# Two-stage ConvFFN in a decoder step: a due-time order of VectorE's work at stage and round changes, a new opening with the norm's sums in job 0 and the last squares summed on TensorE

## The chip, the cores and the metric

One core of one Trainium2 chip runs the whole step. The metric is the device time of one execution in microseconds, the median of several. Names in the profile: PE (TensorE), DVE (VectorE), ACT (ScalarE), POOL (GpSimd), SP (the queue that issues the DMAs).

## The reference

Two layers of a decoder trunk for 1024 prompt tokens and 8 x 8 sample tokens (1088 columns, model width 1024), in float32. Layer 0 has an attention and RG-LRU mixer, layer 1 a chunked mixer; after each mixer stands the part that the change touches:

```python
def rmsnorm(x, g):
    y = xf * lax.rsqrt(jnp.mean(xf * xf, axis=-1, keepdims=True) + EPS)
    return (y * g.astype(jnp.float32)).astype(x.dtype)
...
def conv_ffn(xn, buf, w_g, w_u, w_c, b_c, w_d):
    g = xn @ w_g                                   
    gc, new_buf = causal_dwconv(g, buf, w_c, b_c)  
    return (jax.nn.gelu(gc) * (xn @ w_u)) @ w_d, new_buf
```

`yp = yp + f_p` adds the result to the residual x. The norm's gain is folded into x before the products, its scale `rsqrt(...)`, one number per column, comes after them (`rms_scale`).

## The kernel before, in words

Activations lie with the model width on the partitions (8 tiles of 128 x 1088) and the tokens on the free axis. A float32 operand is split into two fp32r parts, `hi` (rounded, by ACT) and `lo` (the rest, by DVE or POOL), and a product is hi x hi + lo x hi + hi x lo on PE.

**Jobs and products.** An FFN (`class Ffn`) is 40 jobs. Jobs 0 to 23 are stage one: job 2t is a pair of 128 output rows of the gate projection, job 2t+1 the same pair of the up projection. Jobs 24 to 39 are stage two (the down projection): 4 rounds (a round has 6 of the 24 hidden tiles) of 4 quarters (2 output tiles each). Every job is a 2 x 2 block product done with 7 block products instead of 8; their names are `B21, B11, T1, T2, B22, NT4, T3` (0 to 6). The x side of T1, T2, NT4 and T3 are sums of quarters of x, and the weight side are the block sums S1 to S4. A product is 24 matmuls of 128 x 128 x 272 in stage one and 18 in stage two (all L2159, `multiply`), into one of three bank pairs d, a, bb of PSUM; so products wait until the earlier content of their bank is added out.

**Who does what behind PE.** ACT rounds the weight blocks (`block_hi`, L2255), copies bank groups to SBUF (`copy_out`, L2274), does conv bias, gelu (L2303) and the hi parts of the pieces. DVE makes block sums (`block_sum`, L2095) and block low parts (`block_lo`, L2099), adds the other groups (`add_out`, L2466), does the gate scaling by `rms_scale` (`scale_gate`, L2472), the conv taps (L2481), hidden tiles (L2501) and sums (L2511), low parts of the hidden pieces in stage two (`piece_lo`, L2110) and the residual additions (`add_residual`, L2530). POOL does block low parts 0, 1, 5, scales the gelu's result (`gate_scale`, L2105) and adds up the squares (`add_squares`, L1661). Each engine's order is written out by hand; semaphores carry all dependences, and DVE waits in order.

**Opening.** `Output` computes the mixer's output projection, tile by tile (m = 0 to 7), in 12 us each, adds it to x (`vector`, L1828, "evacuation") and spills x to DRAM (`spill_tile`). The first job of the FFN needs all tiles: the B operands (`tile_act`, `tile_dve`, L2393) and the T sums (`open_dve`, `opening_dve`: L2418 for T1, L2398 for T3, L2404 for T2, L2436 for NT4), then hi (ACT) and lo (`part_lo`, L2427 and, on POOL, L2119 and L2124). The squares of the eight tiles are added on POOL into one array, whose column sums are three fp32 matmuls with a matrix of ones (`sums_pe`, L1669); roots follow on ACT (`roots_act`). The product order of job 0 is B11, B21, T1, T2, sums 0 and 1, B22, sum 2, NT4, T3.

**Change of stage.** In stage one x lies in DRAM and its SBUF space holds gate, conv and up tiles. The last hidden pair is finished by DVE at the end of job 24 (`down_first`); SP stores it, then reloads x:

```python
        for g in range(7, 11):
            self.load_piece(sp, g)
        self.store_hidden(sp, PAIRS - 1)
        sp.wait_ge(self.hc, 16 * PAIRS)
        self.reload(sp, 2)
        ...
        self.reload(sp, 3)
        for r in range(ROUNDS):
            ...
            self.load_next(sp, n + 4 * r + 3)
```

The last line with r = 0 loads the w_down block of job 27. In an ordinary job n of stage two DVE first makes S1 and S2 of job n + 1 (`next_sums`), and then adds residual 0, 1, ... of job n. PE's fourth product (T2) of a job waits for residual 1 of the same job, since both use bank a; the first of the next job waits for residual 5.

**Round change.** In the last quarter of a round (jobs 27, 31, 35) and the first of the next (28, 32, 36) DVE also makes the 7 low parts of the next round's hidden pieces.

## Time and profile before

| what | us |
|---|---|
| median of 3 runs | 2572.05 (2571.69 to 2580.36) |
| the profiled execution's own time | 2573.28 |
| its span in the trace | 2571.6 |
| PE busy | 2462.0 (96%) |
| DVE busy | 1769.5 (69%) |
| ACT busy | 1149.9 (45%) |

PE is nearly always busy, so time can only be gained where it is not, or where its granted clock is low. Stretches are given in microseconds from the start of the span. FFN 0 runs from about 590 to 1437, FFN 1 from about 1710 to the end.

### The profile page before, as it was taken

What the parts mean: (1) busy time and instruction counts of PE and PEld (TensorE: products, weight loads), DVE (VectorE), ACT (ScalarE), POOL (GpSimd) and SP (SyncE); (2) the same over time, 40 slices, a digit from 0 to 9 for tenths busy, and PEclk for the clock granted to TensorE, in tenths of its full rate; (3) what the DMA queues carried; (4) which work ended last, traced back from release to release, by engine and by line L of the source; (5) the groups of instructions that cost most, each with busy time, mean ns of one, the idle gap of its engine ahead of it and who ended that gap; (6) DMA issues with size and microseconds to landing.
All of it is one profiled execution on the core that took longest, in us unless ns stands there. A gap on an engine that the chain in (4) does not pass through costs nothing.

```text
span 2571.6 us, 46180 instructions
## 1 busy us (share of the span) xinstructions
PE 2462.0 (96%) x18693; PEld 2361.4 (92%) x18693; DVE 1769.5 (69%) x2158; ACT 1149.9 (45%) x1851; POOL 959.7 (37%) x623
## 2 busy tenths in 40 slices
PE   7999998899899999998999999998999999989998
PEld 7888786589899999998999999997999999989998
DVE  7466557645877777778778443637878787787775
ACT  5565756533544444443334433525444444443331
POOL 3234333214445453542223411334545454532221
PEclk9999999999899999999999999999999999999999
DMA  5101116852222222336443111122232322265422
GB/s 183 52 27 51 40 29 209 270 192 77 84 102 94 98 102 90 111 125 231 141 141 93 47 49 37 52 75 85 91 116 85 107 93 98 89 235 196 140 89 83
DMA packets 214177, 276.99 MB, mean 108 GB/s; under 512 B 11437, under 2 KB 158998, under 8 KB 210894
## 3 DMA queue, kind: packets, MB, share of 16 engines
q1 hardware_dynamic: 212910, 271.83, 31.7%
q8 instruction: 149, 2.44, 0.4%
q10 hardware_dynamic: 576, 2.10, 0.2%
q14 instruction: 62, 0.51, 0.1%
q0 software_dynamic: 480, 0.11, 0.0%
HBM read 203.57 MB, written 70.43 MB: 107 GB/s over the span
## 4 chain that ended last, share of the span: by engine, by line
PE 64%; DVE 9%; issue 3%; ACT 1%; POOL 1%; DMA 1%; DVEq 0%; ACTq 0%; POOLq 0%
PE psum_all L2159 52%; PE psum_all L2823 7%; PE psum_all L148 3%; DVE down_x_ffn L2110 2%; DVE psum_all L2095 1%; DVE x_residual L2530 1%; DMA w_raw<-in_w_gate_dram 1%; PE psum_all L2875 0%; PE psum_all L2839 0%; POOL rms_scale L1661 0%; DVE x_residual L2481 0%; POOL w_lo_part L113 0%; DVE ffn_x_sums L2418 0%; DVE ffn_x_sums L2404 0%; DVE blocks_down L2099 0%
## 5 line engine op out<-in xcount | busy, mean ns | idle before, releaser
L2159 PE MATMUL psum_all<-ffn_x,blocks 128*128 128x272 f32 x5760 | 736.7, 289 | 24.1 <-DVE ffn_x L2427 13.1
L2159 PEld LDWEIGHTS psum_all<-ffn_x,blocks 128*128 128x128 f32 x5760 | 730.1, 189 | 25.7 <-issue 15.0
L2159 PE MATMUL psum_all<-down_x_ffn,blocks_down 128*128 128x272 f32 x2880 | 375.8, 291 | 25.1 <-DVE x_residual L2530 21.5
L2159 PEld LDWEIGHTS psum_all<-down_x_ffn,blocks_down 128*128 128x128 f32 x2880 | 369.1, 191 | 28.3 <-issue 28.1
L2274 ACT COPY x_residual<-psum_all 128x544 f32<-128x544 f32 x192 | 117.9, 614 | 372.9 <-PE psum_all L2159 369.5
L113 POOL TENSOR_TENSOR w_lo_part<-w_raw,w_hi_part 128x1024 fp32r<-128x1024 f32 x52 | 126.9, 2440 | 355.8 <-ACT w_hi_part L97 355.7
L2530 DVE TENSOR_TENSOR x_residual<-x_residual,psum_all 128x544 f32<-128x544 f32 (+1 forms) x224 | 178.4, 798 | 117.8 <-PE psum_all L2159 116.7
L2481 DVE SCALAR_TENSOR_TENSOR x_residual<-x_residual,ffn_params 128x1088 f32<-128x1088 f32 x96 | 215.0, 2240 | 0.0
L2105 POOL TENSOR_TENSOR x_residual<-x_residual,rms_scale 128x1088 f32<-128x1088 f32 x48 | 152.9, 3185 | 151.8 <-ACT x_residual L2303 151.8
L2466 DVE TENSOR_TENSOR x_residual<-x_residual,psum_all 128x544 f32<-128x544 f32 x144 | 130.3, 905 | 91.4 <-PE psum_all L2159 89.5
L2099 DVE TENSOR_TENSOR blocks<-psum_all,blocks 128x512 fp32r<-128x512 f32 x144 | 99.2, 689 | 122.1 <-ACT blocks L2255 122.1
L2823 PE MATMUL psum_all<-operand_a,w_hi_part 128*128 128x364 f32 (+1 forms) x672 | 169.9, 330 | 0.0
L909 PE MATMUL psum_all<-in_hi_even,w_hi_part 128*128 128x384 f32 (+1 forms) x456 | 157.0, 344 | 1.1 <-DVE xb_padded L1430 0.6
L1363 POOL TENSOR_TENSOR take_then_weights<-take_then_weights,x_residual 128x511 f32<-128x511 f32 (+3 forms) x96 | 96.1, 1012 | 156.9 <-DVE x_residual L1395 116.7
L2159 PE MATMUL psum_all<-ffn_x,block_a 128*128 128x272 f32 x1152 | 152.0, 287 | 1.3 <-ACT rms_scale L1676 1.3
L2159 PE MATMUL psum_all<-ffn_x,block_s 128*128 128x272 f32 x1152 | 151.8, 287 | 0.0
L909 PE MATMUL psum_all<-in_lo_even,w_hi_part 128*128 128x384 f32 (+1 forms) x456 | 149.3, 327 | 0.0
L2159 PEld LDWEIGHTS psum_all<-ffn_x,block_a 128*128 128x128 f32 x1152 | 146.9, 188 | 2.4 <-issue 2.4
L909 PE MATMUL psum_all<-in_hi_even,w_lo_part 128*128 128x384 f32 (+1 forms) x456 | 149.1, 327 | 0.0
L2159 PEld LDWEIGHTS psum_all<-ffn_x,block_s 128*128 128x128 f32 x1152 | 146.9, 188 | 0.0
L1395 DVE TENSOR_TENSOR_SCAN x_residual<-x_residual,all_ones 128x512 f32<-128x512 f32 (+3 forms) x96 | 91.9, 991 | 73.2 <-ACT x_residual L1183 73.2
L2511 POOL TENSOR_TENSOR x_residual<-x_residual 128x544 f32<-128x544 f32 x88 | 130.0, 1477 | 6.3
(361 smaller groups left out, 4632.6 us busy)
## 6 DMA issues: line engine op xcount, KB each, us to landing
staging_ffn<-hidden_spill SPq DMA_DIRECT2D x54, 816.0 KB, 5.0
hidden_spill<-x_residual SPq DMA_DIRECT2D x24, 1088.0 KB, 4.0
w_raw<-in_w_gate_dram SPq DMA_DIRECT2D x24, 1024.0 KB, 5.4
x_residual<-in_w_up_dram SPq DMA_DIRECT2D x24, 1024.0 KB, 5.2
pages<-in_cache_k_dram SPq DMA_DIRECT2D x64, 256.0 KB, 3.7
pages<-in_cache_v_dram SPq DMA_DIRECT2D x64, 256.0 KB, 4.5
x_spill<-x_residual SPq DMA_DIRECT2D x24, 546.0 KB, 5.5
x_residual<-x_spill SPq DMA_DIRECT2D x24, 546.0 KB, 6.2
```

The costliest lines, as they stand in the source:

```text
L113: pool.tensor_tensor(dst if dst is not None else self.lo[:, par, :], self.raw[:, par, :], (hi if hi is not None else self.hi[:, par, :]).b ...
L909: mm = pe.matmul(bank(key, 0, b - a), wt[:, n % 2, col], xt[:, k, a:b], start=k == 0 and s == 0, stop=k == KT - 1 and s == 2)
L1363: pool.tensor_tensor(t[:, 0:n - 1], t[:, 0:n - 1], k[:, 1:n], ALU.mult).then_inc(weighted, 1)
L2099: eng.tensor_tensor(self.block(n, i, 1).rearrange("p (q c) -> p q c", c=P), self.source(n, i), self.block(n, i, 0).bitcast(F32).rearrange( ...
L2105: pool.tensor_tensor(self.conv[:, r, :], self.conv[:, r, :], self.core.rb[:, 0:USED], ALU.mult).then_inc(self.gr_ready, 1)
L2159: mm = pe.matmul(self.core.ps[:, b + h, 0:HB], wt[:, q * P:(q + 1) * P], xt[:, q, HB * h:HB * (h + 1)], start=first and at == 0, stop=at = ...
L2274: act.copy(self.half(self.target(n, r), h).rearrange("p (h n) -> p h n", h=2), self.group(name)).then_inc(self.act_out, 1)
L2466: dve.tensor_tensor(dst, dst, src, ALU.add).then_inc(self.dve_out, 1)
L2481: o.did(dve.scalar_tensor_tensor(gc, gb[:, j:j + USED], par[:, f + FT * j:f + FT * j + 1], gc, ALU.mult, ALU.add))
L2511: eng.tensor_tensor(dst, x, y, op).then_inc(self.hsum, 1)
L2530: dve.tensor_tensor(dst, dst, src, ALU.add).then_inc(self.dve_out, 1)
L2823: mm = pe.matmul(self.core.ps[:, self.lane_bank(f), 0:width(c)], wm[:, is_u, col], xm[:, k, chunk(c)], start=k == 0 and s == 0, stop=k == ...
```

## The change

1. **Squares.** The squares of tiles 6 and 7 go to a second array (`late_sq`), those of tile 7 are not added on POOL but by PE: each sum is a matmul of the total and one or two of the last squares, into one bank. Three fp32 matmuls become seven.
2. **Opening.** The product order of job 0 is B11, T1, B21, B22, sums 0 and 1, T2, NT4, sum 2, T3. DVE evacuates tile 6 after two block sums instead of after six block operations; it evacuates tile 7 behind T1's low part. The low parts of T1 and T3, which POOL shared, are all DVE's. Products with `made_first` wait for their low part only at their third group of matmuls. SP spills tiles 4 and 5 ahead of the gate weights of job 0. The waits for all spills become waits for pairs of tiles.
3. **Stage change.** `down_first` goes; job 24 and every first job of a round are `turned_job`, the last of a round `turn_job`. The last hidden tiles and sums are spread over job 25 (`last_hidden`), and both gate scalings of the last pair stand on POOL behind block part 5 in job 24.
4. **Round change.** The low parts of B22, NT4 and T3 come before S1 and S2 of the following job; block low parts 4 and 6 go into the job after.

Of `opening_act`, `open_dve` and `opening_dve` the diff below has the new lines alone.

```diff
...
     def square(self, act, m):
         if m >= 2:
             act.wait_ge(self.s_sum, m - 1)
-        act.activation(self.core.rb[:, 0:USED] if m == 0 else self.sq[:, 0:USED], self.core.x[:, m, 0:USED], ACT.Square
-                       ).then_inc(self.s_sq, 1)
+        act.activation(halves(self.core.rb[:, 0:USED]) if m == 0 else self.square_at(m),
+                       halves(self.core.x[:, m, 0:USED]), ACT.Square).then_inc(self.s_sq, 1)
...
                 self.ffn.spill_tile(sp, m - 4)
+        self.ffn.spill_tile(sp, 4)
+        self.ffn.spill_tile(sp, 5)
         sp.wait_ge(w.s_lo, n0 + KT + 2)
         self.ffn.load(sp, 0)
-        for m in range(4, KT):
-            self.ffn.spill_tile(sp, m)
+        self.ffn.spill_tile(sp, 6)
+        self.ffn.spill_tile(sp, 7)
...
     def vector(self, dve):
         for m in range(KT):
             if m == KT - 2:
-                self.ffn.first_weights_dve(dve)
-            elif m == KT - 1:
-                self.ffn.open_dve(dve)
+                self.ffn.block_sum(dve, 0, "S1")
+                self.ffn.block_sum(dve, 0, "S2")
             dve.wait_ge(*self.job_done(m))
             tile = chunks(self.core.x[:, m, :])
             dve.tensor_tensor(tile, tile, self.bank(m)[:, :, 0:CH], ALU.add).then_inc(self.evac, 1)
-            self.ffn.tile_dve(dve, m, KT - 1)
+            if m < KT - 2:
+                self.ffn.tile_dve(dve, m)
+            elif m == KT - 2:
+                self.ffn.open_dve(dve)
...
+    def square_at(self, m):
+        return self.mem.late_sq if m >= KT - 2 else super().square_at(m)
+
+    def sum_bank(self, c):
+        return self.banks["bb"] if c == 2 else self.banks["d"] + c
+
+    def sums_pe(self, pe, which):
+
+        late = self.square_at(KT - 1)
+        pe.wait_ge(self.s_sum, KT - 2)
+        pe.wait_ge(self.s_sq, KT)
+        for c in which:
+            out = self.core.ps[:, self.sum_bank(c), 0:width(c)]
+            pe.matmul(out, self.core.ones[:, :], self.core.rb[:, chunk(c)], start=True, stop=False,
+                      skip_group_check=True)
+            a, b = c * CH, c * CH + width(c)
+            for h in range(2):
+                lo, hi = max(a, HALF * h), min(b, HALF * (h + 1))
+                if lo < hi:
+                    mm = pe.matmul(out[:, lo - a:hi - a], self.core.ones[:, :], late[:, h, lo - HALF * h:hi - HALF * h],
+                                   start=False, stop=True, skip_group_check=True)
+            mm.then_inc(self.s_mm, 1)
...
-    FIRST_PIECES = {(-1, 4): (B21, B11), (-1, 5): (T1,), (-1, 6): (T2,), (0, 1): (NT4,), (0, 2): (T3,)}
+    FIRST_PIECES = {(-1, 4): (B21, B11), (-1, 5): (T1,), (-1, 6): (T2,), (0, 1): (NT4, T3)}
...
     def sync(self, sp):
-        sp.wait_ge(self.x_out, 16 * KT)
-        sp.wait_ge(self.sum_lead, self.T_MADE[NT4][0])
+        self.x_out(sp, 1)
+        sp.wait_ge(self.sum_lead, self.T_MADE[NT4][1])
         self.load(sp, 1)
...
         self.add_squares(pool, KT - 2)
-        pool.wait_ge(self.act_lead, self.T_HI[T1])
-        pool.tensor_tensor(self.operand(0, T1, 1)[:, 0:2], self.temp(T1)[:, 0:2],
-                           self.operand(0, T1, 0)[:, 0:2].bitcast(F32), ALU.subtract).then_inc(self.t1_lo, 1)
-        self.add_squares(pool, KT - 1)
         self.block_lo(pool, 0, 5)
-        pool.wait_ge(self.act_lead, self.T_HI[T3])
-        pool.tensor_tensor(self.operand(0, T3, 1)[:, 0:2], self.temp(T3)[:, 0:2],
-                           self.operand(0, T3, 0)[:, 0:2].bitcast(F32), ALU.subtract).then_inc(self.t3_lo, 1)
         for n in range(JOBS):
             t = n // 2
             up, last = n < JOBS1 and n % 2, n == JOBS - 1
             for i in range(7):
                 if not last and i in (0, 1, 5):
                     self.block_lo(pool, n + 1, i)
-                if up and (i == 3 or i == 5 and n < JOBS1 - 1):
+                if up and n < JOBS1 - 1 and i in (3, 5):
                     self.gate_scale(pool, t, (i - 3) // 2)
-                elif n == JOBS1 and i == 1:
+                elif n == JOBS1 and i == 5:
+                    self.gate_scale(pool, PAIRS - 1, 0)
                     self.gate_scale(pool, PAIRS - 1, 1)
                 if up and i == 6 and n < JOBS1 - 1:
                     self.hidden_sum(pool, t, T1)
...
+        made_first(T1)
+        pe.wait_ge(self.b_lo, 11)
+        pe.wait_ge(*self.lo_ready(0, 0))
+        self.multiply(pe, 0, 0)
+        pe.wait_ge(self.b_lo, 12)
+        pe.wait_ge(*self.lo_ready(0, 4))
+        pe.wait_ge(self.act_out, 1)
+        self.multiply(pe, 0, 4)
+        pe.wait_ge(self.act_out, 2)
+        self.sums_pe(pe, (0, 1))
         pe.wait_ge(self.dve_out, 1)
-        self.multiply(pe, 0, 3)
-        pe.wait_ge(self.act_out, 1)
-        self.sums_pe(pe, (0, 1))
-        pe.wait_ge(*self.lo_ready(0, 4))
-        pe.wait_ge(self.b_lo, 12)
-        pe.wait_ge(self.act_out, 2)
-        self.multiply(pe, 0, 4)
+        made_first(T2)
+        pe.wait_ge(self.s_root, 2)
+        made_first(NT4)
+        pe.wait_ge(self.dve_out, 2)
         self.sums_pe(pe, (2,))
-        pe.wait_ge(*self.lo_ready(0, 5))
...
+        for i in range(3):
             self.block_hi(act, 0, i)
+        self.tile_hi(act, KT - 2)
+        self.block_hi(act, 0, 3)
         act.wait_ge(self.out.freed, 1)
         for q in range(4):
+            self.even_copy(act, T1, q, 0)
+        act.wait_ge(self.s_sum, KT - 3)
+        self.block_hi(act, 0, 4)
         act.wait_ge(self.out.freed, 2)
+        self.even_copy(act, T3, 0, 1)
+        self.even_copy(act, T3, 1, 1)
+        self.sum_hi(act, T1)
+        self.even_copy(act, T3, 2, 1)
+        self.even_copy(act, T3, 3, 1)
+        self.square(act, KT - 2)
         act.wait_ge(*self.out.job_done(KT - 1))
         self.block_hi(act, 0, 5)
+        self.tile_hi(act, KT - 1)
         self.block_hi(act, 0, 6)
+        self.square(act, KT - 1)
+        self.copy_out(act, 0, 2)
         self.copy_out(act, 0, 0)
+        self.sum_hi(act, T2)
+        self.sum_hi(act, NT4)
+        self.roots_act(act, (0, 1))
...
+    def open_dve(self, dve):
         self.block_lo(dve, 0, 2)
+        self.tile_dve(dve, KT - 2)
         self.block_sum(dve, 0, "S4")
         self.block_lo(dve, 0, 3)
         self.block_sum(dve, 0, "S3")
         for q in range(4):
+            self.t1_sum(dve, q)
+        self.t3_sum(dve, 0)
+        self.t3_sum(dve, 1)
+        self.t2_sum(dve, 0)
+        self.block_lo(dve, 0, 4)
+        self.sum_lo(dve, T1)
+
+    def opening_dve(self, dve):
+        self.nt4_sum(dve, 0)
+        self.tile_lo(dve, KT - 1, 0, B21, 0)
+        self.t3_sum(dve, 2)
+        self.t3_sum(dve, 3)
+        self.tile_lo(dve, KT - 1, 1, B22, 1)
+        for q in (1, 2, 3):
             self.t2_sum(dve, q)
+        for q in (1, 2, 3):
+            self.nt4_sum(dve, q)
         self.add_out(dve, 0, 1)
+        self.sum_lo(dve, T2)
+        self.sum_lo(dve, NT4)
         self.block_lo(dve, 0, 6)
+        self.add_out(dve, 0, 4)
+        self.sum_lo(dve, T3)
...
+    def turn_job(self, dve, n, r):
+
+        self.next_sums(dve, n + 1)
+        self.add_residual(dve, n, 0)
+        self.add_residual(dve, n, 1)
+        self.piece_lo(dve, r + 1, B21)
+        self.add_residual(dve, n, 2)
+        self.piece_lo(dve, r + 1, B11)
+        self.next_lo(dve, n + 1, 2)
+        self.add_residual(dve, n, 3)
+        self.next_lo(dve, n + 1, 3)
+        self.add_residual(dve, n, 4)
+        self.next_lo(dve, n + 1, 4)
+        self.add_residual(dve, n, 5)
+        self.piece_lo(dve, r + 1, T1)
+        self.add_residual(dve, n, 6)
+        self.piece_lo(dve, r + 1, T2)
+
+    def turned_job(self, dve, n, r):
+
+        if r == 0:
+            self.piece_lo(dve, 0, T1)
+        self.add_residual(dve, n, 0)
+        if r == 0:
+            self.piece_lo(dve, 0, T2)
+        self.block_lo(dve, n, 6)
+        self.add_residual(dve, n, 1)
+        self.piece_lo(dve, r, B22)
+        self.add_residual(dve, n, 2)
+        self.piece_lo(dve, r, NT4)
+        self.add_residual(dve, n, 3)
+        self.piece_lo(dve, r, T3)
+        self.block_sum(dve, n + 1, "S1")
+        self.add_residual(dve, n, 4)
+        self.block_sum(dve, n + 1, "S2")
+        self.add_residual(dve, n, 5)
+        self.next_lo(dve, n + 1, 2)
+        self.add_residual(dve, n, 6)
+        self.next_lo(dve, n + 1, 3)
+
+    def last_hidden(self, dve, i):
+        t = PAIRS - 1
+        if i < 2:
+            self.hidden_tile(dve, t, i)
+        elif i < 4:
+            for k in ((T1, T3), (T2, NT4))[i - 2]:
+                self.hidden_sum(dve, t, k)
...
```

The order of the built programs shows three places. The first is DVE's opening of FFN 0, from the last block sums to the evacuation of tile 7 (L1828 before, L1843 now; `ffn_x_sums_7973` is T1, `_7974` T3, `_7975` T2, `_7976` NT4). Before:

```order
L2099 TENSOR_TENSOR blocks<-psum_all,blocks 128x512
L2095 TENSOR_TENSOR psum_all<-w_raw,psum_all 128x512
L2099 TENSOR_TENSOR blocks<-psum_all,blocks 128x512
L2095 TENSOR_TENSOR psum_all<-w_raw 128x512
L1828 TENSOR_TENSOR x_residual<-x_residual,psum_all 128x1092
L2393 SCALAR_TENSOR_TENSOR ffn_x_7964<-x_residual,params,ffn_x_7964 128x544
L2418 SCALAR_TENSOR_TENSOR ffn_x_sums_7973<-x_residual,params,ffn_x_sums_7973 128x544 x4
L2398 SCALAR_TENSOR_TENSOR ffn_x_sums_7974<-x_residual,params,ffn_x_sums_7974 128x544 x3
L2404 SCALAR_TENSOR_TENSOR ffn_x_sums_7975<-x_residual,params,ffn_x_sums_7974 128x544 x3
L1828 TENSOR_TENSOR x_residual<-x_residual,psum_all 128x1092
L2393 SCALAR_TENSOR_TENSOR ffn_x_7963<-x_residual,params,ffn_x_7963 128x544
```

Now:

```order
L1843 TENSOR_TENSOR x_residual<-x_residual,psum_all 128x1092
L2144 TENSOR_TENSOR blocks<-psum_all,blocks 128x512
L2439 SCALAR_TENSOR_TENSOR ffn_x_7964<-x_residual,params,ffn_x_7964 128x544
L2140 TENSOR_TENSOR psum_all<-w_raw,psum_all 128x512
L2144 TENSOR_TENSOR blocks<-psum_all,blocks 128x512
L2140 TENSOR_TENSOR psum_all<-w_raw 128x512
L2455 SCALAR_TENSOR_TENSOR ffn_x_sums_7973<-x_residual,params,ffn_x_sums_7973 128x544 x4
L2444 SCALAR_TENSOR_TENSOR ffn_x_sums_7974<-x_residual,params,ffn_x_sums_7974 128x544 x2
L2450 SCALAR_TENSOR_TENSOR ffn_x_sums_7975<-x_residual,params,ffn_x_sums_7974 128x544
L2144 TENSOR_TENSOR blocks<-psum_all,blocks 128x512
L2468 TENSOR_TENSOR ffn_x_7966<-ffn_x_sums_7973,ffn_x_7966 128x2176
L1843 TENSOR_TENSOR x_residual<-x_residual,psum_all 128x1092
```

The evacuation of tile 6 has moved ahead of four block operations; that of tile 7 had ten tile sums ahead of it, and has now seven, a block part and T1's whole low part (L2468).

The second is DVE in jobs 24 to 26 of FFN 0, around the last hidden tiles (L2501, now L2554) and sums (L2511, now L2564); L2530, now L2583, are residual additions, L2095, now L2140, block sums. Before:

```order
L2530 TENSOR_TENSOR x_residual<-x_residual,psum_all 128x1088
L2099 TENSOR_TENSOR block_s_7980<-psum_all,block_s_7980 128x384
L2501 TENSOR_TENSOR x_residual<-x_residual 128x1088 x2
L2511 TENSOR_TENSOR x_residual<-x_residual 128x544 x4
L2095 TENSOR_TENSOR psum_all<-w_raw 128x384
L2095 TENSOR_TENSOR psum_all<-psum_all,w_raw 128x384
L2530 TENSOR_TENSOR x_residual<-x_residual,psum_all 128x544 x3
L2099 TENSOR_TENSOR blocks_down<-psum_all,blocks_down 128x384
L2095 TENSOR_TENSOR psum_all<-w_raw,psum_all 128x384
```

Now, with the two sums of job 27 and the residuals of job 26 behind them:

```order
L2554 TENSOR_TENSOR x_residual<-x_residual 128x1088
L2583 TENSOR_TENSOR x_residual<-x_residual,psum_all 128x544
L2554 TENSOR_TENSOR x_residual<-x_residual 128x1088
L2583 TENSOR_TENSOR x_residual<-x_residual,psum_all 128x544
L2564 TENSOR_TENSOR x_residual<-x_residual 128x544 x2
...
L2583 TENSOR_TENSOR x_residual<-x_residual,psum_all 128x544
L2564 TENSOR_TENSOR x_residual<-x_residual 128x544 x2
...
L2140 TENSOR_TENSOR psum_all<-pair_raw_ffn_7992 128x384
L2140 TENSOR_TENSOR psum_all<-psum_all,pair_raw_ffn_7992 128x384
L2583 TENSOR_TENSOR x_residual<-x_residual,psum_all 128x544 x3
```

Tiles and sums are spread between the residuals 0 to 3 of job 25; the sums from `pair_raw_ffn` (job 27's w_down) stand in front of job 26's residuals, as they did.

The third is DVE at the first round change, job 28. Before:

```order
L2110 TENSOR_TENSOR down_x_ffn_7990<-staging_ffn_7989,down_x_ffn_7990 128x1632
L2530 TENSOR_TENSOR x_residual<-x_residual,psum_all 128x544
L2110 TENSOR_TENSOR down_x_ffn_7990<-staging_ffn_7989,down_x_ffn_7990 128x1632
L2095 TENSOR_TENSOR psum_all<-pair_raw_ffn_7991 128x384
L2095 TENSOR_TENSOR psum_all<-psum_all,pair_raw_ffn_7991 128x384
L2530 TENSOR_TENSOR x_residual<-x_residual,psum_all 128x544
L2110 TENSOR_TENSOR down_x_ffn_7990<-staging_ffn_7989,down_x_ffn_7990 128x1632
L2099 TENSOR_TENSOR blocks_down<-psum_all,blocks_down 128x384
```

Now:

```order
L2155 TENSOR_TENSOR down_x_ffn_7991<-staging_ffn_7990,down_x_ffn_7991 128x1632
L2583 TENSOR_TENSOR x_residual<-x_residual,psum_all 128x544
L2155 TENSOR_TENSOR down_x_ffn_7991<-staging_ffn_7990,down_x_ffn_7991 128x1632
L2583 TENSOR_TENSOR x_residual<-x_residual,psum_all 128x544
L2155 TENSOR_TENSOR down_x_ffn_7991<-staging_ffn_7990,down_x_ffn_7991 128x1632
L2140 TENSOR_TENSOR psum_all<-pair_raw_ffn_7992 128x384
L2583 TENSOR_TENSOR x_residual<-x_residual,psum_all 128x544
L2140 TENSOR_TENSOR psum_all<-psum_all,pair_raw_ffn_7992 128x384
```

The low part of T3 (the last L2110, now L2155) was behind two block sums and stands now ahead of them.

## Rows read from the trace of the kernel before

**Rows 1.** Waits of PE: line, who released it, us in total, times, longest.

```profile
...
PE psum_all L2159 <- DVE x_residual L2530: 21.5, 12, 4.7
PE psum_all L2159 <- DVE ffn_x L2427: 13.1, 2, 6.8
...
PE psum_all L2159 <- DVE down_x_ffn L2110: 8.9, 9, 1.4
```

**Rows 2.** Chain that ended last: start, us, what; the weights' load, stage one of both FFNs.

```profile
...
617.68 6.63 DMA w_raw<-in_w_gate_dram
...
701.62 451.29 PE psum_all L2159 x3609
...
1821.91 451.28 PE psum_all L2159 x3609
```

**Rows 3.** Timeline of PE, opening of FFN 0: start, us, what, matmuls, [idle before <-releaser].

```profile
...
637.86 3.18 PE L2159 MATMUL psum_all<-ffn_x,blocks 128*128 128x272 f32 x24
646.01 8.32 PE L2159 MATMUL psum_all<-ffn_x,blocks 128*128 128x272 f32 x48 [4.98 <-DVE x_residual L1828]
660.63 4.86 PE L2159 MATMUL psum_all<-ffn_x,blocks 128*128 128x272 f32 x24 [6.30 <-DVE ffn_x L2427]
665.33 1.39 PE L1669 MATMUL psum_all<-rms_scale,all_ones 128*128 128x364 f32 x4
...
677.05 15.16 PE L2159 MATMUL psum_all<-ffn_x,blocks 128*128 128x272 f32 x120
```

**Rows 4.** Busy time by windows: stretch, then PE, PEld, DVE, ACT, POOL, PEclk, DMA.

```profile
...
625.00:665.00 40.00, 28.73 (x173) 28.32 (x172) 34.77 (x34) 21.53 (x26) 15.41 (x7) 0.83 0.26 91
```

**Rows 5.** Timeline of DVE, opening of FFN 0.

```profile
...
638.28 2.17 DVE L2398 SCALAR_TENSOR_TENSOR ffn_x_sums<-x_residual,params,ffn_x_sums 128x544 f32<-128x544 f32 x3
...
661.74 2.42 DVE L2427 TENSOR_TENSOR ffn_x<-ffn_x_sums,ffn_x 128x2176 fp32r<-128x2176 f32 x1
...
678.47 1.29 DVE L2472 TENSOR_TENSOR x_residual<-x_residual,rms_scale 128x1088 f32<-128x1088 f32 x1
...
685.11 0.71 DVE L2466 TENSOR_TENSOR x_residual<-x_residual,psum_all 128x544 f32<-128x544 f32 x1
```

**Rows 6.** Timeline of PE, first round change (jobs 28 and 29).

```profile
...
1250.37 2.42 PE L2159 MATMUL psum_all<-down_x_ffn,block_a 128*128 128x272 f32 x18
1253.66 2.49 PE L2159 MATMUL psum_all<-down_x_ffn,block_s 128*128 128x272 f32 x18 [0.88 <-DVE down_x_ffn L2110]
1257.15 8.01 PE L2159 MATMUL psum_all<-down_x_ffn,blocks_down 128*128 128x272 f32 x62 [1.00 <-DVE x_residual L2530]
```

**Rows 7.** Timeline of DVE, first round change: T3's low part.

```profile
...
1251.67 1.85 DVE L2110 TENSOR_TENSOR down_x_ffn<-staging_ffn,down_x_ffn 128x1632 fp32r<-128x1632 f32 x1
```

**Rows 8.** Timeline of PE, change of stage (jobs 25 and 26).

```profile
...
1196.28 4.02 PE L2159 MATMUL psum_all<-down_x_ffn,blocks_down 128*128 128x272 f32 x18 [4.67 <-DVE x_residual L2530]
...
1207.55 11.43 PE L2159 MATMUL psum_all<-down_x_ffn,blocks_down 128*128 128x272 f32 x90
```

**Rows 9.** Timeline of DVE, change of stage.

```profile
...
1171.69 3.60 DVE L2110 TENSOR_TENSOR down_x_ffn<-staging_ffn,down_x_ffn 128x1632 fp32r<-128x1632 f32 x1
...
1209.42 0.56 DVE L2095 TENSOR_TENSOR psum_all<-pair_raw_ffn 128x384 f32<-128x384 f32 x1
```

**Rows 10.** Timeline of POOL, change of stage: the second gate scaling.

```profile
...
1170.71 2.86 POOL L2105 TENSOR_TENSOR x_residual<-x_residual,rms_scale 128x1088 f32<-128x1088 f32 x1
```

**Rows 11.** Timeline of SP, change of stage: the DMA issues.

```profile
...
1193.64 0.32 SPq L1993 DMA_DIRECT2D hidden_spill<-x_residual  x1
1197.66 1.90 SPq L1985 DMA_DIRECT2D x_residual<-x_spill  x4
1199.67 0.46 SPq L1968 DMA_DIRECT2D pair_raw_ffn<-in_w_down_dram  x1
```

**Rows 12.** DMA issues: of the page, and of 1197 to 1212: KB, median us to landing.

```profile
...
x_spill<-x_residual SPq DMA_DIRECT2D x24, 546.0 KB, 5.5
...
pair_raw_ffn<-in_w_down_dram SPq DMA_DIRECT2D x1, 768.0 KB, 9.2
```

256 lines of the change are left out of this document (100 added, 156 removed).

## The prediction

> **What bounds the kernel now.** I read the waits of TensorE (PE) first, then the chain that ended last, then the timelines of the places that the two name. PE is the bound nearly everywhere: between the opening and the last job of stage one it runs 451.3 us without a break, in both FFNs [rows 2]. The change touches neither those stretches nor the two mixers, so all it can move is what PE loses where one regime turns into another. The waits [rows 1] put that loss on VectorE (DVE), in three kinds of places in each of the two FFNs:
>
> - the opening (job 0): PE waits 13.1 us in two times for the low part of a tile sum (L2427), and in each FFN 5.0 us for the evacuation of the last tile (L1828) [rows 1, 3];
> - the change of stage (jobs 24 and 25) and the round changes (into jobs 28, 32, 36): 21.5 us behind residual additions (L2530) and 8.9 us behind low parts of the hidden pieces (L2110).
>
> All sums below are against the profiled execution's own time, 2573.3 us (span 2571.6 us), 1.2 us above the median of the three runs, 2572.05. The second FFN repeats the first with a shift of 1120.3 us [rows 2], so I work out the first and double it. A run of this kernel can be told from no change at about 0.5%, 12.9 us.
>
> **Opening.** At full clock a product of 24 matmuls takes 3.0 us (0.125 each), so job 0 is 21 us of products. It takes 39.2 us, from 637.86 to 677.05 [rows 3]: two idles of 4.98 and 6.30 us, and after each the matmuls run slowly: 48 in 8.32 us where 6.2 would do, 24 in 4.86 instead of 3.16. The mean granted clock of 625 to 665 is 0.83, that is, part at 2.4 and part at 1.2 GHz [rows 4]; it fell after the idles, and the slow stretches cost 2.1 + 1.7 us.
>
> The new order, walked with the durations of rows: a tile sum 0.72 us on DVE when undisturbed, a whole low part 2.4 (2.3 from start to start) [rows 5].
>
> - DVE has the weights' S1 and S2 at 625.7 (624.3 and two operations of 0.7), and has evacuated tile 6 by about 627.4, ahead of the other block work. B11's low part, S4, two block parts and S3 are done near 632.0. Four T1 sums, two T3 sums, one T2 sum, a block part and T1's low part take it to about 640.1, and the last tile's evacuation ends at 641.4, where it ended at 646.0.
> - PE runs B11 from 637.9 to 640.9, waits 0.6 us for that evacuation, and runs T1 (to 644.5), B21 (647.5), B22 (650.5). The sums of squares follow. Two fp32 matmuls are four instructions in 1.39 us, some 0.61 each matmul [rows 3]. There were three; now there are seven, with the length of six. So 2.4 us behind B22 and 1.2 before T3, **1.8 us more PE work**, all of it on PE's path.
> - T2 (to 656.0) needs a low part that is done at 652.7, NT4 (659.0) one at 655.1, T3 starts at 660.2 and ends at 663.2; its low part is ready at 660.3 and is asked for 2.0 us into the product. Job 0 ends **13.9 us earlier** than at 677.05. POOL's last squares addition (the seventh) is gone, since PE adds those squares; it only made DVE wait.
> - Then DVE is behind. After job 0 it still owes add_out 6 and five block operations before the first gate scaling (L2472), which I put at 668.0: 4.8 us after job 1's start, against 1.4 us before (678.47 after 677.05). From there to the end of add_out(1,1) it needs 7.3 us (678.47 to 685.11 + 0.71) [rows 5], so job 1's fourth product starts at 675.4 instead of 686.05. The gain that is left is **10.7 us**; the other 3.2 turn into a new wait in job 1.
> - The gate weights of job 0 (first needed by S1) now stand on SP's queue behind the spills of tiles 4 and 5. They landed 6.63 us after 617.68 [rows 2]. Tile 5 is evacuated, and so spilled, at about 615.4; such a spill takes 5.5 us to land [rows 12], until 620.9, 3.2 us after the weights' issue. The bounds are 0 and 3.2; I take 0.7, near the lower, since the weights are not waited for by PE itself and the two transfers overlap.
>
> By the Trainium skill (DMA: Bandwidth & Descriptors, HWDGE ordering) each DMA engine consumes its descriptors in ring order and a completion increment lands only after every earlier write of that engine, which speaks against putting spills ahead of weights; by it the term would be the upper bound; no row before shows a spill ahead of that load.
>
> Opening: 10.7 - 0.7 = **10.0 us each, 20 together** (bounds 4 and 13 each).
>
> **Round changes.** Job 28's sixth product starts at 1250.37, and two products of 2.25 us later, at 1254.9, job 29 could start; it starts at 1257.15 [rows 6]: 2.3 us lost, 0.88 idle for T3's low part, 1.00 for residual 5, the rest at their edges. DVE is busy throughout, and in front of both stand S1, S2 and S4 of job 29, which nobody needs yet. Now T3's low part (1.85 us [rows 7]) starts after residual 3, about 1249.8, and is done by 1251.7 to 1252.4, when 1252.6 is due; residual 5 ends near 1254.2 for 1254.9. What is pushed back (two block low parts) is due nine microseconds on. Late next would be residual 1 of job 29: 1261.1 for 1261.6. The six changes lose 2.1 to 2.5 us each, 14.2 in all; I take **13** (bounds 5 and 14.2), leaving 0.2 each for edges.
>
> **Change of stage.** Three waits shrink, and one takes their place.
>
> - Gone: the gate scaling beside DVE's taps, S1 and S2 ahead of three low parts, the hidden sums in one block ahead of residual 1 of job 25 (4.67 us of PE idle before 1196.28 and 4.02 us for 18 matmuls that take 2.5 [rows 8]). I get job 25 started at 1177.7 instead of 1184.7.
> - But both gate scalings now run on POOL one behind the other in job 24, after block part 5 of job 25, about 1181.4 to 1187. A DVE operation with both operands in SBUF stalls beside one: 3.60 us [rows 9] for 1.85 [rows 7], next to a gate scaling of 2.86 [rows 10]. S1 of job 26 and the first hidden tile meet them. Counting on, residual 1 of job 25 ends near 1188.8 and the last hidden sum, now behind residual 3, near **1195.4. Before, it was 1193.6** [rows 11].
> - On that sum hangs a chain on SP that the change leaves alone: store of the hidden sums (landed 4.0 us later), four reloads of x, then w_down for job 27, issued at 1199.67 and 9.2 us on the way [rows 11, 12]. So these weights land 15.2 us after the last hidden sum, at 1208.9. S1 of job 27 (1209.42 [rows 9]) stands on DVE ahead of *all* residuals of job 26. Before, nobody felt it: job 26 began at 1207.55 [rows 8] and its residual 1 was due at 1214.3.
> - Now job 26 begins near 1199.9, its residual 1 is due at 1206.6, and the weights land at 1195.4 + 15.2 = 1210.6. With S1, S2, residuals 0 and 1 (2.5 us) PE resumes at 1213.1 after 6.5 us idle, then loses 1.6 us to the low clock, as after 4.67 us. Job 26 ends at 1223.7; before, 1207.55 + 15.77 = 1223.3.
>
> So the seven microseconds won in job 24 are given back: **0.4 us slower**, in the second FFN 0.8 (its job 26 ended 0.4 earlier). Sum +1. Every microsecond of the last hidden sum counts fully here, down to a gain of 10.5 each if the chain did not bind; the bounds of the sum itself (1192 to 1198) give -3.5 to +3 each.
>
> **Sum:** -20 - 13 + 1 = -32: 2573.3 - 32 = **2541 us**.
>
> **Rivals.**
>
> *A, the stage change pays in full.* If w_down for job 27 were not waited for (a faster landing, or hidden sums by 1188), nothing else is late in job 26 but 1 to 3 us behind residual 1 of job 25: about 10 us each, 2541 - 21 = 2520. For it: the DVE rows of job 25 that I take as disturbed might not be. Against: 15.2 us from store to landing is one measured chain, and 3 MB pass in it. 14%; half-way cases lie inside the forecast.
>
> *B, late gate weights.* The opening's first DVE operation waits for them and every later one moves with it. If they don't start before tile 5's spill has landed, it is 3.2 us instead of 0.7 in each: 2541 + 5 = 2546 (this is what the Trainium skill's page above would make of it); with the new waits of ScalarE (two hi parts, a table load and two roots in a row before T3's) a further 3 each: 2552. 20%.
>
> *C, round changes stay.* If T3's piece lands late from DRAM, its low part is as late as before and the order gains only residual 5: 1 us each, 2541 + 7 = 2548. Against: at the round changes PE's waits name DVE and no transfer [rows 1, 6]. 8%.
>
> *D, slower than before.* B's place with a larger delay: S1 and S2 stand ahead of tile 6's evacuation on DVE, and all of the opening behind it, so weights d us later cost 2d over both FFNs. That eats the sum at d = 16 and is slower by over 0.5% from d = 22.5; at d = 24 it gives 2541 + 48 = 2589. Nothing in the rows makes half a megabyte cost that. 3%.
>
> *E, no effect that can be measured*: the opening's DVE debt eats its gain, as 3.2 us of it already do, and A's wait is longer than I think: 2562. 5%.
>
> **How the numbers follow.** The forecast, with its own spread of 2532 to 2550, has 50%; A 14, B 20, C 8, D 3, E 5. The likeliest is 2541. A range of 2523 to 2556 holds the forecast, B, C and the half-way cases to A, and leaves out A's far half, D and E. Faster by over 0.5% (under 2559): 0.91. Within 0.5%: 0.06. Slower: 0.03.
>
> **What would show it.** Opening: job 0 ends 25 us after its first matmul, at full clock, one idle under 1 us in it, and a new wait of about 3 us before job 1's fourth product behind add_out (the DVE line of L2466). Rounds: no PE idle above 0.4 us there. Stage: job 24 in about 16.8 us; then two idles, some 4 us in job 25 and some 6 us in job 26, the second ended by residual 1 with S1's wait for the w_down DMA ahead of it on DVE. If that second idle is missing, A holds; if job 0's first product is not followed by tile 7's evacuation by 642, B or D does; if the idles at the rounds stand, C.

## The result, and the profile after

| what | before | after |
|---|---|---|
| median, us | 2574.35 (2571.69 to 2580.36, 4 runs) | 2558.19 (2556.99 to 2559.26, 4 runs) |
| the profiled execution: own time, span | 2573.28, 2571.6 | 2559.26, 2557.5 |
| PE busy, granted clock over the span | 2462.0, 0.992 | 2469.9, 0.990 |

The ratio is 0.9941 (95% interval 0.9928 to 0.9954), in a second measurement of the same kernel 0.9928 (0.9915 to 0.9942; 2557.71 against 2576.85). So the change is faster, by 16 to 19 us, where I had forecast 32. 2558 lies above my range (2523 to 2556). One execution among the experiments (`b_w27_before`) took 4830.59 us, nearly twice as long as its ten others, and is left out of its ratio.

The waits of PE in the changed kernel (engine, line, releaser: us in total, times, longest). L2196 is `multiply`, L2583 a residual addition, L2519 `add_out`:

```profile
PE psum_all L2196 <- DVE x_residual L2583: 24.9, 10, 7.3
PE psum_all L2196 <- DVE x_residual L2519: 10.7, 2, 5.4
```

The waits for tile low parts (13.1 us), for the last tile's evacuation (5.0 in each FFN) and for low parts of pieces (8.9) [rows 1, 3] have left the top of the list. Residual additions stand there with 24.9 us instead of 21.5, and two waits of 5.4 us for `add_out` are new.

**Opening.** PE, then DVE, then POOL at the new wait in FFN 0 (start, us, line, what, matmuls or operations, [idle before <-releaser]; all timelines below have the same columns):

```profile
666.35 9.16 PE L2196 MATMUL psum_all<-ffn_x,blocks 128*128 128x272 f32 x72
680.87 7.89 PE L2196 MATMUL psum_all<-ffn_x,blocks 128*128 128x272 f32 x48 [5.36 <-DVE x_residual L2519]
```

```profile
671.66 2.38 DVE L2525 TENSOR_TENSOR x_residual<-x_residual,rms_scale 128x1088 f32<-128x1088 f32 x1
...
676.50 2.34 DVE L2525 TENSOR_TENSOR x_residual<-x_residual,rms_scale 128x1088 f32<-128x1088 f32 x1
...
680.02 0.71 DVE L2519 TENSOR_TENSOR x_residual<-x_residual,psum_all 128x544 f32<-128x544 f32 x1
...
682.10 0.32 DVE L2545 TENSOR_SCALAR x_residual<-gate_sample,ffn_params 128x64 f32<-128x64 f32 x1
```

```profile
671.37 1.53 POOL L2144 TENSOR_TENSOR block_a<-x_residual,block_a 128x512 fp32r<-128x512 f32 x1 [5.60 <-ACT block_a L2289]
...
676.42 1.26 POOL L2144 TENSOR_TENSOR blocks<-w_raw,blocks 128x512 fp32r<-128x512 f32 x1 [1.22 <-ACT blocks L2289]
```

The stretch of the last 48 matmuls by itself (window, PE, PEld, DVE, ACT, POOL busy, then granted clock, DMA share, GB/s):

```profile
680.87:688.60 7.73, 7.73 (x48) 7.73 (x49) 6.17 (x10) 3.50 (x6) 0.00 (x0) 0.76 0.00 0
```

Job 0 ends 25.2 us after the output's end (the output projection's last product, 641.13) and PE idles 0.25 us in it; before, it took 39.2 [rows 3]. Then job 1's fourth product waits 5.36 us, and 48 matmuls take 7.89 us where 6.2 would do, at a granted clock of 0.76. Ahead of the awaited `add_out` at 680.02 stand on DVE two gate scalings of 2.38 and 2.34 us; before, the first took 1.29 [rows 5]. Each began while POOL made a block low part: POOL's ended at 672.90 and DVE's at 674.04, POOL's at 677.68 and DVE's at 678.84: each 1.1 to 1.2 us later, near the 1.29 us that a gate scaling would take if it began only when POOL's operation has ended.

**Round change.** DVE, POOL and PE around the start of job 29:

```profile
1253.07 1.00 DVE L2140 TENSOR_TENSOR psum_all<-pair_raw_ffn 128x384 f32<-128x384 f32 x1
...
1255.18 1.42 DVE L2140 TENSOR_TENSOR psum_all<-w_raw 128x384 f32<-128x384 f32 x1
...
1257.11 2.17 DVE L2583 TENSOR_TENSOR x_residual<-x_residual,psum_all 128x544 f32<-128x544 f32 x3
```

```profile
1252.63 1.01 POOL L2144 TENSOR_TENSOR block_a<-pair_raw_ffn,block_a 128x384 fp32r<-128x384 f32 x1 [6.56 <-ACT block_a L2289]
1255.16 1.01 POOL L2144 TENSOR_TENSOR blocks_down<-w_raw,blocks_down 128x384 fp32r<-128x384 f32 x1 [1.52 <-ACT blocks_down L2289]
```

```profile
1251.08 6.92 PE L2196 MATMUL psum_all<-down_x_ffn,blocks_down 128*128 128x272 f32 x54
1258.79 3.38 PE L2196 MATMUL psum_all<-down_x_ffn,blocks_down 128*128 128x272 f32 x25 [0.79 <-DVE x_residual L2583]
```

PE runs from job 28 into job 29 without a break; the 0.88 and 1.00 us of [rows 6] are gone. But job 29's fourth product waits 0.79 us for residual 1, in front of which stand two weight sums, the first 1.42 instead of 0.57 us, again beside POOL. So was the sum at 1253.07, with 1.00. At the other round changes this wait is 0.3 to 1.3 us.

**Change of stage.** PE, SP and DVE in FFN 0:

```profile
1184.09 4.42 PE L2196 MATMUL psum_all<-down_x_ffn,blocks_down 128*128 128x272 f32 x18 [3.71 <-DVE x_residual L2583]
...
1207.87 7.31 PE L2196 MATMUL psum_all<-down_x_ffn,blocks_down 128*128 128x272 f32 x36 [4.54 <-DVE x_residual L2583]
```

```profile
1190.77 0.32 SPq L2038 DMA_DIRECT2D hidden_spill<-x_residual  x1
1194.78 1.87 SPq L2030 DMA_DIRECT2D x_residual<-x_spill  x4
1196.75 0.55 SPq L2013 DMA_DIRECT2D pair_raw_ffn<-in_w_down_dram  x1
```

```profile
1205.12 0.57 DVE L2140 TENSOR_TENSOR psum_all<-pair_raw_ffn 128x384 f32<-128x384 f32 x1 [6.75 <-DMA pair_raw_ffn<-in_w_down_dram]
```

This is the chain that I had walked: hidden sums stored at 1190.77, reloads at 1194.78 when the store has landed, weights of job 27 asked for at 1196.75. S1 of job 27 idles 6.75 us for them on DVE, with residuals 0 and 1 of job 26 behind it, and PE stands 4.54 us in FFN 0, 7.30 in FFN 1. In FFN 1 the first step of the chain is longer, the store of the last hidden sums:

```profile
2304.59 0.32 SPq L2038 DMA_DIRECT2D hidden_spill<-x_residual  x1
2310.57 1.89 SPq L2030 DMA_DIRECT2D x_residual<-x_spill  x4
```

It takes 6.0 us there, and 4.0 in FFN 0 and in both FFNs of the kernel before. In FFN 1 of the other kernels below that have the new order of the stage change it takes 4.7 to 6.4 us, but 4.0 in `f4_second_job` and `g1_rows_copy_first`, where job 25 is ordered anew. Why is open.

A measure that I use below is the time from one job's sixth product (block_a) to another's; "job 0's mark" is the start of job 0's sixth product. In stage one it is 21.00 us a job, in stage two 15.77.

| stretch of that measure | before | after | after again | opening only | stage and rounds only |
|---|---|---|---|---|---|
| start to job 0 | 670.97 | 659.14 | 655.42 | 657.02 | 671.78 |
| jobs 23 to 27, FFN 0 | 79.89 | 80.19 | 79.57 | 80.31 | 80.25 |
| jobs 27 to 39, FFN 0 | 196.44 | 193.20 | 193.38 | 195.74 | 191.92 |
| jobs 2 to 23, FFN 1 | 441.00 | 443.94 | 443.94 | 441.00 | 441.00 |
| jobs 23 to 27, FFN 1 | 79.48 | 81.65 | 82.08 | 78.68 | 81.20 |
| jobs 27 to 39, FFN 1 | 201.00 | 196.31 | 196.55 | 200.57 | 196.12 |

### The profile page after: what moved, and what is told of

Same layout as the page of the kernel before. It is cut to its first block, busy times and chain, and to the rows that moved or that the text cites. A ratio compares the mean times of both kernels' runs of the same rounds, so it can differ in the third digit from the quotient of the medians.

```text
span 2557.5 us, 46222 instructions
## 1 busy us (share of the span) xinstructions
PE 2469.9 (97%) x18709; PEld 2370.0 (93%) x18709; DVE 1763.2 (69%) x2158; ACT 1147.5 (45%) x1849; POOL 945.7 (37%) x617
## 4 chain that ended last, share of the span: by engine, by line
PE 67%; DVE 7%; issue 2%; DMA 1%; ACT 1%; SPq 0%; DVEq 0%; ACTq 0%
PE psum_all L2196 52%; PE psum_all L2889 7%; PE psum_all L153 6%; DVE psum_all L2140 1%; DVE x_residual L2583 1%; DVE down_x_ffn L2155 1%; DMA pair_raw_ffn<-in_w_down_dram 1%; PE psum_all L2941 0%; PE psum_all L2905 0%; DVE ffn_x L2468 0%; DMA hidden_spill<-x_residual 0%; DMA staging_ffn<-hidden_spill 0%; DVE blocks_down L2144 0%; PE psum_all L2929 0%; PE psum_all L2733 0%
## 5 line engine op out<-in xcount | busy, mean ns | idle before, releaser
L2196 PE MATMUL psum_all<-ffn_x,blocks 128*128 128x272 f32 x5760 | 734.7, 288 | 11.2 <-DVE x_residual L2519 10.7
L2196 PEld LDWEIGHTS psum_all<-ffn_x,blocks 128*128 128x128 f32 x5760 | 728.7, 189 | 12.0 <-issue 11.0
L2196 PE MATMUL psum_all<-down_x_ffn,blocks_down 128*128 128x272 f32 x2880 | 377.2, 291 | 24.9 <-DVE x_residual L2583 24.9
L2196 PEld LDWEIGHTS psum_all<-down_x_ffn,blocks_down 128*128 128x128 f32 x2880 | 370.5, 191 | 27.3 <-issue 26.9
L2583 DVE TENSOR_TENSOR x_residual<-x_residual,psum_all 128x544 f32<-128x544 f32 (+1 forms) x224 | 178.0, 797 | 95.4 <-PE psum_all L2196 93.5
L2534 DVE SCALAR_TENSOR_TENSOR x_residual<-x_residual,ffn_params 128x1088 f32<-128x1088 f32 x96 | 209.8, 2186 | 0.0
L2519 DVE TENSOR_TENSOR x_residual<-x_residual,psum_all 128x544 f32<-128x544 f32 x144 | 130.3, 905 | 88.7 <-PE psum_all L2196 86.8
L2196 PE MATMUL psum_all<-ffn_x,block_s 128*128 128x272 f32 x1152 | 152.8, 288 | 0.0
L2196 PE MATMUL psum_all<-ffn_x,block_a 128*128 128x272 f32 x1152 | 152.2, 288 | 0.0
L2196 PEld LDWEIGHTS psum_all<-ffn_x,block_s 128*128 128x128 f32 x1152 | 147.5, 188 | 0.5
L2196 PEld LDWEIGHTS psum_all<-ffn_x,block_a 128*128 128x128 f32 x1152 | 147.4, 188 | 0.0
L2564 POOL TENSOR_TENSOR x_residual<-x_residual 128x544 f32<-128x544 f32 x88 | 129.8, 1475 | 6.3
```

Of the source, the lines that this page charges most:

```text
L2196: mm = pe.matmul(self.core.ps[:, b + h, 0:HB], wt[:, q * P:(q + 1) * P], xt[:, q, HB * h:HB * (h + 1)], start=first and at == 0, stop=at = ...
L2519: dve.tensor_tensor(dst, dst, src, ALU.add).then_inc(self.dve_out, 1)
L2534: o.did(dve.scalar_tensor_tensor(gc, gb[:, j:j + USED], par[:, f + FT * j:f + FT * j + 1], gc, ALU.mult, ALU.add))
L2564: eng.tensor_tensor(dst, x, y, op).then_inc(self.hsum, 1)
L2583: dve.tensor_tensor(dst, dst, src, ALU.add).then_inc(self.dve_out, 1)
```

## The experiments

Ratios are against the kernel before, measured on the same chip, with a 95% interval. "After" is the changed kernel.

### The kernel again, and its two halves

`a_again` is the changed kernel. `p_open` has the new opening and the old order of stage two; `p_down` the reverse. From `p_open`'s edit against the changed kernel:

```diff
 vector, p_open:
-        for n in range(JOBS1, JOBS):
+        self.down_first(dve)
+        for n in range(JOBS1 + 1, JOBS):
...
-    FIRST_PIECES = {(-1, 4): (B21, B11), (-1, 5): (T1,), (-1, 6): (T2,), (0, 1): (NT4, T3)}
+    FIRST_PIECES = {(-1, 4): (B21, B11), (-1, 5): (T1,), (-1, 6): (T2,), (0, 1): (NT4,), (0, 2): (T3,)}
```

> The changed kernel once more. The stretches that the change touches sum to -20.3 us in the first pair of profiles (openings -14.9, round changes -8.1, stage changes +2.7), but the span fell by 14.1 only: 3.2 us went in the mixers ahead of the first FFN (its output's job 7 ended at 641.1 for 637.9) and 3.0 in the product jobs of the second FFN's first stage. Theory V (these 6 us are differences between executions, not made by the change): this profile has the output's end anywhere from 637 to 642 and a ratio between 0.9922 and 0.9945. Rival S (the change makes them, by where its code or its buffers lie): the output's end again at 641 or later, the second FFN's jobs 1 to 23 again 2.5 to 3 us longer than the first kernel's, ratio 0.994.

> Only the new opening, with the order of the second stage as before. By the profile the openings give 7.3 and 7.6 us: ratio 0.9942 (2557). My forecast had them at 10.0 each, 0.9922 (2552). If the openings' gain were given back further on, the ratio would be above 0.996. The wait at job 1's fourth product should be 5.3 us again.

> Only the new order around stage and round changes, with the opening as before. By the profile -8.1 for the six round changes and +2.7 for the two stage changes: -5.4, ratio 0.9979 (2566.6). My forecast had -13 and +1.2: 0.9954. If the round changes' gain is eaten by the new wait behind residual 1 alone, the idle time there is 0.8 to 1.3 us at each; rival, that the orders of the stage change cost more than they show: ratio at or over 1.000.

Measured: again 0.9928 (0.9915 to 0.9942); opening only 0.9949 (0.9935 to 0.9963), 2562.62; stage and rounds only 0.9967 (0.9956 to 0.9978), 2567.93. The halves give 13 and 8.5 us, 21.6 together, against 18.5 for the whole. The intervals (3 us or so each way) cover the difference, so nothing shows that they take anything from each other. The wait in job 1 was 5.36 us again. In `p_down` the round changes gave 4.5 and 4.9 us, the stage changes cost 0.4 and 1.7.

Theory V holds for the time ahead of the FFNs: the output's end, where job 0 begins, lies at 641.1 in one profile of the changed kernel and at 637.4 in the other (job 0's mark at 659.1 and 655.4). The two profiles differ in a stretch of the mixer that the change leaves alone (window, PE, PEld, DVE, ACT, POOL busy, then granted clock, DMA share, GB/s; first the changed kernel, then the same again):

```profile
400.00:541.00 141.00, 119.10 (x1460) 84.50 (x1454) 82.54 (x118) 75.04 (x142) 33.91 (x39) 0.96 0.75 249
```

```profile
400.00:541.00 141.00, 118.13 (x1477) 83.72 (x1472) 84.05 (x120) 77.81 (x145) 33.97 (x39) 0.99 0.74 250
```

The clock was 0.96 in the one and 0.99 in the other, as in the kernel before. Of the 2.9 us in FFN 1's first stage these two profiles could not tell; that comes below.

### Job 27's weights asked for early

```diff
+        self.load_next(sp, n + 3)
         self.store_hidden(sp, PAIRS - 1)
...
-            self.load_next(sp, n + 4 * r + 3)
+            if r:
+                self.load_next(sp, n + 4 * r + 3)
```

> The weights of job 27 are asked for ahead of the last hidden stores and the reload of x, and no longer behind them. Theory (the wait before job 26's fourth product, 4.5 and 7.3 us, is the queue: hidden store 4.0, four reloads 1.9, landing 8.3, then the two sums that stand ahead of residual 1 on the vector engine): the wait goes to 0 to 1 us and the time falls by 7 to 12 us against the changed kernel, ratio 0.990 to 0.9915. Rival (the reload of x itself, asked for at 1194.8, sets the residuals of job 26): it lands at 1200 to 1204, the wait shrinks only to 1 to 3 us and the time falls by 4 to 7 us. Second rival (the load slows the stores and reloads that it now runs beside): nothing gained, ratio 0.994.

Measured: 2542.20 us, 0.9867 (0.9846 to 0.9887), 15.5 less than the changed kernel beside it, more than either theory gave. PE and SP of this kernel in FFN 0:

```profile
1181.70 4.02 PE L2198 MATMUL psum_all<-down_x_ffn,blocks_down 128*128 128x272 f32 x18 [3.71 <-DVE x_residual L2585]
...
1192.99 11.43 PE L2198 MATMUL psum_all<-down_x_ffn,blocks_down 128*128 128x272 f32 x90
```

```profile
1174.65 0.37 SPq L2013 DMA_DIRECT2D pair_raw_ffn<-in_w_down_dram  x1
```

Asked for at 1174.65, 18.6 us earlier counted from job 0's mark, the weights are there, and job 26's five products run through (90 matmuls in 11.43 us). In FFN 1 a wait of 0.57 us is left. Jobs 23 to 27 take 71.8 and 74.6 us instead of 79.6 and 82.1: 7.8 and 7.5, since the clock stays high as well. This is my rival A: with the load out of the chain, the stage change pays 8.1 and 4.9 us against before.

The same edit on the kernel before:

> The kernel before, with nothing changed but the place of job 27's weight load on SyncE's queue, ahead of the last hidden stores and of the reload. It tells whether the 15 us that this gives the changed kernel need the new order of the second stage. Theory (in the kernel before, PE waited 4.7 us for a residual that stood behind hidden tiles on the vector engine, and not for this load): at most 1 to 3 us gained, ratio 0.999. Rival (the load alone held the stage change in both): 8 to 15 us, ratio 0.995.

Measured: 1.0004 (0.9995 to 1.0013). Its wait is where it was, and for the same reason [rows 8]:

```profile
1197.98 4.02 PE L2161 MATMUL psum_all<-down_x_ffn,blocks_down 128*128 128x272 f32 x18 [4.67 <-DVE x_residual L2532]
```

So neither the new order nor the early load gains anything at the stage change alone; together they gain 13 us (8.1 and 4.9). Each hid the other's wait.

### The residuals ahead of the sums, at round changes and in job 25

```diff
     if after_turn:
         self.block_lo(dve, n, 4)
         self.block_lo(dve, n, 6)
+    early = after_turn and r > 0
+    if early:
+        self.add_residual(dve, n, 0)
+        self.add_residual(dve, n, 1)
     self.next_sums(dve, n + 1)
     for i in range(7):
-        self.add_residual(dve, n, i)
+        if not early or i > 1:
+            self.add_residual(dve, n, i)
```

> In the second job of rounds 2 to 4 the residual additions 0 and 1 stand ahead of the two weight sums of the next job. Theory (the new wait of 0.8 to 1.3 us at each round change is these two sums, of which one takes 1.4 instead of 0.6 us while the Pool engine makes a low part): the wait goes, and the six round changes give 5 to 7 us more: ratio 0.9905. Rival (the sums that are now later hold up ACT's high part of the next job's third block, needed 4 us later): a wait of its own there, nothing gained, ratio 0.993.

Measured: 2551.87 us, 0.9909 (0.9894 to 0.9924). Jobs 27 to 39 of FFN 0 take 189.47 us, without a wait between them; in FFN 1 193.68. Against the two profiles of the changed kernel that is 3.7 to 3.9 and 2.6 to 2.9 us. The theory holds: with it the six changes give 14.3 us against before, about all that they lost. It shows that the order of the sums and residuals is enough; POOL's part in the wait is read from the rows, not from this run.

In job 25 the same (`r == 0`), on top of the early weights:

> On top of the early weights of job 27: in job 25, too, residuals 0 and 1 ahead of job 26's two sums and of the last hidden tile. Theory (the 3.7 us wait before job 25's fourth product is 4.7 us of sums and hidden tile ahead of residual 1 on the vector engine, two of them slow beside the Pool engine's gate scaling): that wait goes to under 0.5 us and 3 us per FFN are gained, against 2542 for the kernel with the early weights alone: 2536, ratio 0.9842. Rival: the hidden tiles, stores and the reload of x move later by as much, and the wait returns at job 26's fourth product, ratio 0.9867.

Measured: 2544.12, 0.9879 (0.9864 to 0.9894): nothing gained. Jobs 23 to 27 take 74.3 and 75.5 us, 2.5 and 0.9 more than with the early weights alone. The 3.7 us wait went from job 25's fourth product to its fifth, and a smaller one came back in job 26. PE in FFN 0:

```profile
1182.89 4.42 PE L2198 MATMUL psum_all<-down_x_ffn,blocks_down 128*128 128x272 f32 x18 [3.79 <-DVE x_residual L2585]
...
1200.36 4.76 PE L2198 MATMUL psum_all<-down_x_ffn,blocks_down 128*128 128x272 f32 x36 [1.12 <-DVE x_residual L2585]
```

### The opening's debt: order, contention, amount of work

First, the addition that PE waits for goes ahead of job 2's sums, the gate scaling and the tap:

```diff
                 self.block_lo(dve, 1, 4)
                 self.block_lo(dve, 1, 6)
+                self.add_out(dve, u, 1)
             self.block_sum(dve, u + 1, "S1")
...
-            self.add_out(dve, u, 1)
+            if t:
+                self.add_out(dve, u, 1)
```

> In the opening the addition that frees the bank for job 1's fourth product stands ahead of job 2's two sums, the gate scaling of tile 1 and the first tap, as its product was done at 672.5 already. Theory (the 5.4 us wait is the vector engine's order, 9.1 us of other work in front of it): no wait there, no slow clock behind it (48 products in 6.0 instead of 7.9 us), 7 us gained in each FFN, 14 in all against the changed kernel: ratio 0.9875. Rival (the vector engine is short of time as such): the wait comes back at job 1's later products or job 2's and the ratio stays within 0.991 to 0.994.

Measured: 2552.33, 0.9911 (0.9897 to 0.9924). In FFN 0 the one wait has become three:

```profile
674.70 3.25 PE L2196 MATMUL psum_all<-ffn_x,blocks 128*128 128x272 f32 x24 [0.52 <-DVE x_residual L2519]
679.97 3.24 PE L2196 MATMUL psum_all<-ffn_x,blocks 128*128 128x272 f32 x24 [2.01 <-ACT x_residual L2310]
...
694.27 10.99 PE L2196 MATMUL psum_all<-ffn_x,blocks 128*128 128x272 f32 x86 [2.06 <-DVE x_residual L2519]
```

Jobs 0 to 2 take 48.5 us in both FFNs instead of 50.2 to 51.6, 1.7 to 3.0 us less. In FFN 0 most of that is because the matmuls stay at full rate. In FFN 1 they don't: behind the second wait, again 2.01 us, 24 take 4.77 us instead of 3.2, the third wait is only 0.41, and the sum is the same. So something other than these matmuls set the end, and the rival came nearer than the theory. Next, in the changed kernel as it stood, POOL waits for that addition before its next three low parts:

```diff
+                if (n, i) == (0, 5):
+                    pool.wait_ge(self.dve_out, 4)
                 if not last and i in (0, 1, 5):
                     self.block_lo(pool, n + 1, i)
```

> In the opening the Pool engine makes its next three low parts (blocks 5 of job 1, 0 and 1 of job 2) only after the addition that frees the bank for job 1's fourth product. Nothing is left out and the vector engine's order stays. Theory (its scalings and sums took 2.4, 2.3 and 1.8 instead of 1.3, 1.3 and 0.7 us because the Pool engine worked beside them, which is most of why the wait was 5.4 us and not my 3.2): the two gate scalings take 1.3 us each, the wait falls to 3.0 to 3.6 us, 2 to 4 us gained per FFN with what the clock gives back: ratio 0.990. Rival (their length is their own, or the Pool engine is not the cause): scalings again 2.3 us, ratio 0.993.

Measured: 2555.78, 0.9916 (0.9901 to 0.9930). DVE and PE of this kernel:

```profile
670.04 1.29 DVE L2527 TENSOR_TENSOR x_residual<-x_residual,rms_scale 128x1088 f32<-128x1088 f32 x1
...
673.77 1.28 DVE L2527 TENSOR_TENSOR x_residual<-x_residual,rms_scale 128x1088 f32<-128x1088 f32 x1
...
678.31 1.11 DVE L2547 TENSOR_SCALAR x_residual<-gate_sample,ffn_params 128x64 f32<-128x64 f32 x1
```

```profile
677.09 6.28 PE L2198 MATMUL psum_all<-ffn_x,blocks 128*128 128x272 f32 x48 [3.19 <-DVE x_residual L2521]
...
694.96 13.78 PE L2198 MATMUL psum_all<-ffn_x,blocks 128*128 128x272 f32 x96 [2.53 <-DVE x_residual L2521]
```

The gate scalings take 1.29 and 1.28 us and the wait is 3.19 us: the 3.2 of my forecast. So POOL beside DVE was what my walk lacked. The Trainium skill (SBUF — State Buffer, Who interferes with whom) says that a DVE instruction with two SBUF inputs contends with a GpSimd instruction that reads SBUF, and calls what they share an exclusive lock; these rows agree. But jobs 0 to 2 take 51.0 and 49.6 us: at most 1.5 us gained in FFN 1 and nothing clear in FFN 0. POOL's low parts now meet the three small sample operations of tile 0 (1.11 us for the first, which takes 0.32 at 682.10 in the kernel after; 3.6 for the three instead of 0.9), and job 2's second product waits 2.53 us. Last, on top of the addition first, the vector engine gets less to do, by leaving the taps' result out:

```diff
+        if t == 0:
+            o.did(dve.scalar_tensor_tensor(gc[:, 0:16], gb[:, j:j + 16], ..., gc[:, 0:16], ALU.mult, ALU.add))
+            return
```

> The opening's addition first, and the two taps of each of the first two gate tiles cut to 16 of 1088 columns, so that their result is left out: the vector engine has 5 us less to do before job 2's second product. Theory (what is left of the opening's debt, 0.5 + 2.0 + 2.1 us of waits with the addition first and 5.4 + slow clock without, is the vector engine's time as such, whatever its order): the third wait goes from 2.1 us to nothing, and jobs 0 to 2 take 46 to 47 us instead of 48.5 in each FFN. Rival (the waits hang on the chain root, scaling, ACT's first taps and its copies, not on the amount of work): the waits stay at 2.0 and 2.1 us and nothing is gained.

Measured: 2547.67, 0.9892 (0.9876 to 0.9908). Jobs 0 to 2 take 46.2 us in both FFNs, 2.3 less. The third wait is gone; the first two stand as they were:

```profile
676.76 3.25 PE L2196 MATMUL psum_all<-ffn_x,blocks 128*128 128x272 f32 x24 [0.45 <-DVE x_residual L2519]
682.03 3.24 PE L2196 MATMUL psum_all<-ffn_x,blocks 128*128 128x272 f32 x24 [2.02 <-ACT x_residual L2310]
...
691.11 15.16 PE L2196 MATMUL psum_all<-ffn_x,blocks 128*128 128x272 f32 x120
```

So both hold in part. The third wait goes when DVE has less to do; the second (2.0 us) hangs on ACT, whose copy stands behind the first tap of tile 1, which needs its scaling. The run does not tell DVE's amount of work from its meetings with POOL: with the taps gone, the sample operations of tile 1 also miss POOL's gate scaling and take 0.31 and 0.28 us, where with the addition first they took 2.34 and 1.25.

### The spills' place

```diff
-        self.ffn.spill_tile(sp, 4)
-        self.ffn.spill_tile(sp, 5)
         sp.wait_ge(w.s_lo, n0 + KT + 2)
         self.ffn.load(sp, 0)
+        self.ffn.spill_tile(sp, 4)
+        self.ffn.spill_tile(sp, 5)
         self.ffn.spill_tile(sp, 6)
```

> Only the places of two of the eight saving transfers of x on SyncE's queue: tiles 4 and 5 behind the load of job 0's gate weights again, as in the kernel before. My forecast charged 0.7 us per FFN for having them ahead; in the changed kernel the load landed 5.3 us after its issue, against 6.6 before. Theory (they had landed by then and cost nothing): landing 5.3 us or, with the spills now beside it, 6.3 to 6.9, and the time within 2 us of the changed kernel's, ratio 0.993. Rival (the queue's order matters): the landing under 5 us and up to 2 us gained.

Measured: 2558.90, 0.9928 (0.9911 to 0.9944), the same as after. DMA issues between 600 and 640 us (buffers, queue, times, KB each, median us to landing), with the spills ahead (the changed kernel), then behind:

```profile
x_spill<-x_residual SPq DMA_DIRECT2D x3, 546.0 KB, 2.7
w_raw<-in_w_gate_dram SPq DMA_DIRECT2D x1, 1024.0 KB, 5.3
```

```profile
x_spill<-x_residual SPq DMA_DIRECT2D x3, 546.0 KB, 7.3
w_raw<-in_w_gate_dram SPq DMA_DIRECT2D x1, 1024.0 KB, 6.4
```

### Together

The early weights, the addition first, and the residuals first in the second job of every round:

> The early weights, the addition first in the opening, and the residuals first in the second job of every round, together. If the gains add: 2542 - 14 - 6 - 6 = 2516, ratio 0.976; if the vector engine is short of time, 2528 or more, 0.981.

> The combination of three again, beside the new order: ratio 0.981 to 0.984. It also tells how a stretch of unchanged code varies: the jobs of the first stage take 21.00 us each in one FFN and 21.14 in the other in some profiles; in this kernel's first profile it was the second FFN. If the program decides, it is the second again; if the execution decides, it can be either or none.

Measured: 2531.30, 0.9825 (0.9811 to 0.9838), and 2532.26, 0.9831 (0.9817 to 0.9845). That is the sum of the gains as measured one by one (15.5 + 5.4 + 5.8 us off 2557.7 is 2531), and not of those forecast: of the opening's 14 us 5.4 had come, of job 25's 6 none. Then job 25's order by hand; sums of job 26 behind the first hidden sums:

```diff
+    def second_job(self, dve, n):
...
+        self.add_residual(dve, n, 1)
+        self.hidden_tile(dve, t, 0)
+        self.add_residual(dve, n, 2)
+        self.hidden_tile(dve, t, 1)
+        for k in (T1, T3):
+            self.hidden_sum(dve, t, k)
+        self.block_sum(dve, n + 1, "S1")
+        self.block_sum(dve, n + 1, "S2")
+        for k in (T2, NT4):
+            self.hidden_sum(dve, t, k)
+        self.add_residual(dve, n, 3)
```

> On top of the early weights, the opening's addition first and the residuals first in rounds 2 to 4: in job 25 residual 0, residual 1, hidden tile 0, residual 2, hidden tile 1, hidden sums, and job 26's sums only then. Theory (the 3.7 us wait in job 25 moved to its fifth product when only residuals 0 and 1 went ahead, because residual 2 still stood behind the two sums and the hidden tile): no wait over 1 us in job 25, the last hidden sum 2 to 4 us earlier, so that the reload is in time: 2531 - 6 to 9 = 2523, ratio 0.9795. Rival (the Pool engine's gate scalings beside the vector engine set the hidden tiles, whatever the order): the wait stays at 2 us or more, ratio 0.982 to 0.983.

Measured: 2539.47, 0.9856 (0.9841 to 0.9871), a miss. The wait at the fifth product is 0.6 us, but the sixth waits 6.73 for ACT's copy of the state rows, which stood behind a block of job 26 whose sums I had pushed back. PE in FFN 0, and below it the edit that answers it (against this try; the old places of the sums and of the copy go):

```profile
1182.88 2.50 PE L2198 MATMUL psum_all<-down_x_ffn,blocks_down 128*128 128x272 f32 x18 [0.58 <-DVE x_residual L2585]
1192.11 4.42 PE L2198 MATMUL psum_all<-down_x_ffn,block_a 128*128 128x272 f32 x18 [6.73 <-ACT state_rows L2282]
```

```diff
         self.add_residual(dve, n, 2)
+        self.next_sums(dve, n + 1)
         self.hidden_tile(dve, t, 1)
...
+                if m == 1 and i == 2:
+                    self.state_rows_act(act)
                 if n < JOBS - 1:
                     self.block_hi(act, n + 1, i)
```

> The kernel of the last try, in which job 25's sixth product waited 6.7 us for ACT's copy of the state rows: ACT was held by block 2 of job 26, whose sums I had put behind the hidden sums. Now job 26's sums stand behind residual 2, and ACT copies the state rows ahead of blocks 2 and 3 of job 26. Theory (order on ACT and the vector engine, not the gate scaling on the Pool engine, holds job 25): no wait in job 25 over 1 us, jobs 23 to 27 in 69 to 71 us (76.7 in the last try, 72.5 in the combination of three, 71.8 with the early weights alone): 2526, ratio 0.981. Rival (the last hidden tile is set by the Pool engine and the reload behind it by the stores): a wait at job 26's fourth product of 2 us or more, 2531, ratio 0.983.

Measured: **2525.02 us (2523.70 to 2531.21), 0.9805 (0.9791 to 0.9820)**: 51 us under the kernel before, 7 under the combination of three. PE, then DVE's first hidden tile, in FFN 0:

```profile
1180.65 2.49 PE L2198 MATMUL psum_all<-down_x_ffn,blocks_down 128*128 128x272 f32 x18 [0.42 <-DVE x_residual L2585]
...
1187.07 2.50 PE L2198 MATMUL psum_all<-down_x_ffn,block_s 128*128 128x272 f32 x18 [1.67 <-DVE x_residual L2585]
1190.55 11.50 PE L2198 MATMUL psum_all<-down_x_ffn,blocks_down 128*128 128x272 f32 x90 [0.99 <-DVE x_residual L2585]
```

```profile
1176.39 3.48 DVE L2556 TENSOR_TENSOR x_residual<-x_residual 128x1088 f32<-128x1088 f32 x1
```

Jobs 23 to 27 take 70.2 and 70.7 us, and the rival's wait at job 26's fourth product did not come: the order on ACT and DVE had held most of job 25. The theory's "no wait over 1 us" did not hold, since 1.67 us are left in job 25, and 0.99 ahead of job 26. POOL still costs DVE 2.2 us there, as a hidden tile takes 3.48 us beside a gate scaling where two took 2.48 in the kernel before; whether that is what is left is not shown.

## Why the prediction was wrong

- **Opening, forecast 10.0 each; 7.3 and 7.4 in the first profile, 6.2 and 6.6 in the second** (job 2's second product against the output's end; the 7.6 and 14.9 of my expectations are a little too high). Job 0 came as walked: 13.97 us earlier against 13.9. The first gate scaling was forecast at 668.0 and began at 671.66, which is 668.4 with the later output end taken off. The step that failed is "From there to the end of add_out(1,1) it needs 7.3 us". In the kernel before, POOL worked there too, but only the second scaling met it for more than 0.1 us, and when more than half of POOL's operation was over:

```profile
682.20 1.72 DVE L2472 TENSOR_TENSOR x_residual<-x_residual,rms_scale 128x1088 f32<-128x1088 f32 x1
```

```profile
681.47 1.30 POOL L2099 TENSOR_TENSOR blocks<-w_raw,blocks 128x512 fp32r<-128x512 f32 x1 [2.90 <-ACT blocks L2255]
```

  In the new order each scaling begins within 0.3 us of the start of a POOL operation, and the stretch took 9.1 us. The longer wait brought the clock down, 1.7 us more (2.8 in the second profile, where the 48 matmuls take 9.01), for which I had charged nothing although [rows 3] show it behind both idles. `f3_pool_held` shows the cause of the size; it and `e2_add_out_first` also show that putting this right alone gains little, since DVE and ACT are behind through job 2.
- **Gate weights, forecast +0.7 each: the sign was wrong.** They landed 5.3 us after their issue, against 6.6 [rows 2]; with the spills put behind them, 6.4. I had taken the spill as something the load must wait for. But the spill of tile 5, issued at 618.65, landed in 2.7 us, 0.4 us after the load's issue at 620.96; the 5.5 us that I took for it are the median of all spills, and those beside the load take over 7. In these rows what slows the load is what moves beside it. From the Trainium skill's ordering rule (DMA: Bandwidth & Descriptors, Queues, rings and completion order) I had read 3.2 us; with the spill landed, no row here tests it.
- **Round changes, forecast 13; 7.9 in the first profile, 7.5 in the second, 9.4 in `p_down`.** The waits went as forecast. The step that failed is "residual 1 of job 29: 1261.1 for 1261.6". I named it as late next, and counted half a microsecond in hand, with sums of 0.57 us. Beside POOL one took 1.42 and one 1.00, which together is the 1.3 us by which residual 1 ended later than forecast, counted from the job's start (7.5 us for 6.2). `e3_residuals_first` moves the residuals ahead and gets the rest, 14.3.
- **Change of stage, forecast +0.4 and +0.8; +0.3 and +2.2 in the first profile, -0.3 and +2.6 in the second.** The chain is the forecast one: two idles of 3.7 and 4.5 us for "some 4 and some 6", and in FFN 0 the sum came out too. The term that was mis-sized is in FFN 1, the store of the last hidden sums: "landed 4.0 us later", and it took 6.0. With it PE's idle is 7.30 us. Rival A, which I gave 14% as a faster landing, was one moved load away, worth 15 us.
- **The rest of the miss is not the change's.** The terms of the first profile sum to 20.1 us (14.7 + 7.9 - 2.5), from 2573.3 to 2553.2. To its own time, 2559.26, 3.3 us are missing ahead of the FFNs (output's end 641.13 for 637.86) and 2.9 in FFN 1's first stage. Repeats show both to come and go; the medians lie 16 and 19 us below the kernel before. So of the 18 us between forecast and first profile 5.3 are the openings, 5.1 the round changes, 1.5 the stage changes and some 6 neither.

The result lies between the forecast and rival E (2562, 5%), whose first half, DVE's debt eating more of the opening, is what happened. No rival had the round changes' new wait.

The shape of the error is one thing twice, at the opening and at the round changes: durations from rows of operations hardly disturbed, put beside POOL work that the change itself moved there. At the stage change I had priced it (3.60 us for 1.85), and there FFN 0 came out.

## What to carry to other kernels

Where a new order lets DVE and POOL meet, take each DVE duration from a row in which POOL is busy beside it, or, for an operation like the gate scalings here, count its time from the end of POOL's operation. When a long wait is cleared and the next takes its place, ask what stands in front of the awaited instruction on *every* in-order queue (SP's loads, ACT's copies too): here a load and an order were worth nothing alone and 13 us together. And in the opening, where DVE is behind for three jobs, one addition moved ahead repaid 2 to 3 of the 7 us that it promised; its last wait went only when DVE's taps were left out.

## What the runs showed that I had not expected

Stage one runs at one of two rates. PE in FFN 1 of the changed kernel, then of the kernel with early weights, the same five products at a granted clock of 1.00:

```profile
1867.84 15.26 PE L2196 MATMUL psum_all<-ffn_x,blocks 128*128 128x272 f32 x120
```

```profile
1858.20 15.16 PE L2198 MATMUL psum_all<-ffn_x,blocks 128*128 128x272 f32 x120
```

15.26 against 15.16 us: 21.14 for a job instead of 21.00, from the first jobs of a stage to its last, 2.9 us in all. Of 17 profiles 9 have it in one FFN's first stage (7 in the second FFN, 2 in the first), none in both. `best_all` had it there in its first profile and not in its second, so the execution decides, and the kernel before has it too in `b_w27_before`. Stage two has the like: 15.87 for 15.77 in some stretches. What sets it stays open; nothing was tried on it.
